# Routing stage of an expert layer: the router's product turned round, the register loads split around two gathers, fewer filler matmuls, an early Silu table, and the last norm's squares by pairs

## The reference, cut to what matters

```
def _rmsnorm_f32(x, g):
    xf = x.astype(jnp.float32)
    return xf * lax.rsqrt(jnp.mean(xf * xf, axis=-1, keepdims=True) + RMS_EPS) * g.astype(jnp.float32)
...
def _moe_swiglu(h, router_w, router_b, w_gate, w_up, w_down):
    hf = h.reshape(bsz * seq, d)
    logits = (hf @ router_w + router_b).astype(jnp.float32)
    probs = jax.nn.softmax(logits, axis=-1)
    top_p, top_i = lax.top_k(probs, TOP_K)
    top_p = top_p / jnp.sum(top_p, axis=-1, keepdims=True)
    gates = jnp.sum(jax.nn.one_hot(top_i, N_EXPERTS, dtype=jnp.float32) * top_p[..., None], axis=1)
    out = jnp.zeros_like(hf)
    for e in range(N_EXPERTS):
        out = out + gates[:, e:e + 1] * _swiglu(hf, w_gate[e], w_up[e], w_down[e])
    return out.reshape(bsz, seq, d)
```

## Time and profile before

| | us |
|---|---|
| median of 3 runs | 1529.41 |
| lowest, highest | 1526.29, 1532.66 |
| the profiled execution: its time | 1524.15 |
| the profiled execution: its span | 1522.3 |
| TensorE busy (matmuls) | 1437.0, 94% |
| routing, from the last norm's end to the first block | 589.4 to 618.2 |
| expert loop | 618.2 to 1501.8 |
| final sum, norm and output | 1501.8 to 1522.3 |

### The profile page before, as it was taken

One profiled execution on the slowest core, in us unless ns is written; L12 is line 12 of the kernel. 1 busy time (PEld: TensorE's weight loads), 2 busy tenths in 40 slices (PEclk: granted clock), 3 DMA queues, 4 the chain that ended last, 5 costly groups with the idle time before them and its releaser, 6 DMA issues.

```text
span 1522.3 us, 44793 instructions
## 1 busy us (share of the span) xinstructions
PE 1437.0 (94%) x19926; PEld 1087.0 (71%) x19926; DVE 371.7 (24%) x1020; ACT 158.5 (10%) x377; POOL 138.2 (9%) x230
## 2 busy tenths in 40 slices
PE   5998999999998899899999989989989999999997
PEld 4886788888887887666667767757757767765554
DVE  2815240220203714111111111111111111113334
ACT  2103111111012203100000000000000000000001
POOL 0000041240300000000000000000000000000000
PEclk9999999999999998999999999999999999999999
DMA  9948496656318805749999999999999999999860
GB/s 386 422 157 310 173 369 239 266 194 249 139 62 353 333 0 229 298 180 387 425 427 410 426 427 408 427 425 413 426 426 409 420 427 424 420 425 380 366 293 29
DMA packets 44203, 493.92 MB, mean 324 GB/s; under 512 B 4896, under 2 KB 5152, under 8 KB 5792
## 3 DMA queue, kind: packets, MB, share of 16 engines
q1 hardware_dynamic: 41040, 475.02, 76.0%
q10 hardware_dynamic: 3024, 16.73, 2.7%
HBM read 478.10 MB, written 13.63 MB: 323 GB/s over the span
## 4 chain that ended last, share of the span: by engine, by line
PE 81%; DMA 12%; DVE 4%; issue 1%; ACT 1%; POOLq 0%; SPq 0%; POOL 0%; DVEq 0%
PE PS L740 30%; PE PS L442 20%; PE PS L749 15%; DMA ring<-in_expert_stream 9%; PE PS L596 5%; DMA arena<-in_expert_stream 2%; PE PS L426 2%; DMA ring<-in_dense_stream 2%; PE PS L758 1%; DVE arena L1047 1%; PE PS L720 1%; PE PS L650 1%; PE PS L566 1%; PE PS L578 1%; PE PS L474 1%
## 5 line engine op out<-in xcount | busy, mean ns | idle before, releaser
L740 PE MATMUL PS<-ring,arena 128*32 128x256 f32 x7040 | 406.5, 381 | 26.2 <-DMA ring<-in_expert_stream 14.6
L740 PEld LDWEIGHTS PS<-ring,arena 128*32 128x32 f32 x7040 | 257.3, 110 | 154.1 <-issue 20.7
L442 PE MATMUL PS<-arena,ring 128*128 128x256 f32 x1408 | 313.4, 383 | 3.9 <-ACT arena L850 2.7
L442 PEld LDWEIGHTS PS<-arena,ring 128*128 128x128 f32 x1408 | 268.6, 192 | 44.4 <-issue 3.0
L749 PE MATMUL PS<-ring,arena 128*32 128x256 f32 x4928 | 298.3, 380 | 0.8 <-DVE consts L1047 0.8
L749 PEld LDWEIGHTS PS<-ring,arena 128*32 128x32 f32 x4928 | 183.8, 110 | 85.1 <-issue 3.1
L740 PE MATMUL PS<-arena 128*32 128x256 f32 x2816 | 162.1, 380 | 6.9 <-DMA arena<-in_expert_stream 4.8
L1047 DVE TENSOR_TENSOR stat<-stat,PS 128x128 f32<-128x128 f32 x154 | 44.2, 287 | 508.4 <-ACT stat L1004 508.4
L1047 DVE TENSOR_TENSOR arena<-arena,PS 128x256 f32 (+1 forms) x123 | 55.2, 449 | 372.2 <-PE PS L442 232.8
L740 PEld LDWEIGHTS PS<-arena 128*32 128x32 f32 x2816 | 106.3, 110 | 53.8 <-DMA arena<-in_expert_stream 5.8
L1595 POOL COPY arena<-arena 128x256 f32 x153 | 61.3, 401 | 812.6 <-PE PS L740 764.0
(11 more groups left out here) (183 smaller groups left out, 623.8 us busy)
## 6 DMA issues: line engine op xcount, KB each, us to landing
ring<-in_expert_stream SPq DMA_DIRECT2D x136, 2048.0 KB, 19.7
ring<-in_dense_stream SPq DMA_DIRECT2D x105, 1024.0 KB, 7.5
arena<-in_expert_stream SPq DMA_DIRECT2D x32, 2048.0 KB, 22.8
ssm_scratch<-arena ACTq DMA_DIRECT2D x12, 1024.0 KB, 4.9
ring<-ssm_scratch SPq DMA_DIRECT2D x12, 1024.0 KB, 9.7
arena<-in_xt ACTq DMA_DIRECT2D x1, 1024.0 KB, 13.7
arena<-in_ssm_small ACTq DMA_DIRECT2D x1, 1024.0 KB, 9.6
out_t<-arena ACTq DMA_DIRECT2D x4, 256.0 KB, 2.6
```

What stands on the lines that cost most here:

```text
L442: mm = pe.matmul(PS[:, bank, j * T:(j + 1) * T], w[:, c, j * P:(j + 1) * P], moving[:, c, :], start=(c == 0), stop=(c == NC - 1))
L740: mm = pe.matmul(PS[32 * q:32 * q + 32, 0, 0:256], hbuf[:, c * BLK:(c + 1) * BLK], w[:, q * 256:(q + 1) * 256], start=(c == 0), stop=(c == ...
```

## The change

It has five parts.

**Router's product.** The router's 8 columns become the stationary side and the chunk's 256 tokens the moving side: eight matmuls, one for each chunk, into a tile of 8 partitions x 256. DVE copies that to `logit_t` (a stretch of `reps`, free at that time), and TensorE turns it with two small matmuls against the 8 x 8 corner of the identity. The turning of the chunks, which lay between the products, comes behind them: the first four ahead of the turn of the logits, the other twelve behind it, and ACT copies them in the order 0, 1, 2, 3.

**Register loads.** TensorE loads four sums after the first gather and four after the second, instead of eight after the second. ACT loads its eight ahead of its two copies instead of behind them. POOL makes the first copy to `hbuf` when one group is gathered (`hg_ready` 1) instead of two.

**Fillers.** Both spins of nine become spins of three.

**Silu table.** ACT runs a Silu on two columns right behind the Exp of the routing, into a tile that is overwritten later. On DVE the three small steps that turn this Exp into the gates stand behind the `sel` matrices.

**Squares by pairs.** ACT's squares of the final norm wait for `e_x` 1, 2, 3 and 4 one by one, instead of all for 4.

The diff, cut to its core:

```diff
+        logit_t = reps[:, 256:512]
...
             for c in range(NC):
                 pe.wait_ge(h_ready, 3 * NC + c + 1)
-                for tt in range(2):
-                    mm = pe.matmul(PS[:, 5, tt * 8:tt * 8 + 8], H[:, c, tt * P:(tt + 1) * P],
-                                   cols[:, K_RW + 8 * c:K_RW + 8 * c + 8], start=(c == 0 and tt == 0), stop=(c == NC - 1),
-                                   skip_group_check=True)
-                if c == NC - 1:
+                mm = pe.matmul(PS[0:EXPERTS, 5, 0:T], cols[:, K_RW + 8 * c:K_RW + 8 * c + 8], H[:, c, :], start=(c == 0), stop=(c == NC - 1))
+            mm.then_inc(logits_turned, 1)
+            for m in range(4):
+                if m == 1:
+                    pe.wait_ge(logits_taken, 1)
+                    for tt in range(2):
+                        mm = pe.matmul(PS[:, 2, 32 + 8 * tt:40 + 8 * tt], logit_t[0:EXPERTS, tt * P:(tt + 1) * P], ident[0:EXPERTS, 0:EXPERTS],
+                                       start=True, stop=True)
                     mm.then_inc(logits_ready, 1)
-                for tt in range(2):
-                    m, i = (tt * NC + c) // 4, c % 4
+                for i in range(4):
+                    tt, c = (4 * m + i) // NC, (4 * m + i) % NC
                     mm = pe.transpose(PS[:, (6, 7, 0, 1)[m], i * P:(i + 1) * P], H[:, c, tt * P:(tt + 1) * P], ident)
-                    if i == 3:
-                        mm.then_inc(htm_psum, 1)
+                mm.then_inc(htm_psum, 1)
...
-            spin(9, 3)
+            spin(3, 3)
             pe.wait_ge(htm_ready, 4)
             gather(0)
+            pe.wait_ge(items_ready, 1)
+            upto = blocks_upto(pe, range(EXPERTS // 2))
             gather(1)
-            pe.wait_ge(items_ready, 1)
-            upto = blocks_upto(pe)
+            upto += blocks_upto(pe, range(EXPERTS // 2, EXPERTS))
...
-            spin(9, 2)
+            spin(3, 2)
             sums(4, 0)
...
             act.activation(r2[5], r2[4], ACT.Exp).then_inc(pick_exp, 1)
+            act.activation(e_act_b[:, 0:2], r2[4], ACT.Silu)
...
+            act.wait_ge(items_ready, 1)
+            upto = blocks_upto(act)
             take_gathered(0)
             take_gathered(1)
-            act.wait_ge(items_ready, 1)
-            upto = blocks_upto(act)
...
-            act.wait_ge(e_x, 4)
-            squares(4, lambda cp: None)
+            squares(4, lambda cp: act.wait_ge(e_x, cp + 1))
...
+            dve.wait_ge(logits_turned, 1)
+            dve.tensor_copy(logit_t[0:EXPERTS], PS[0:EXPERTS, 5, 0:T]).then_inc(logits_taken, 1)
             dve.wait_ge(logits_ready, 1)
-            link(tt(logit, PS[:, 5, 0:16], cols[:, K_RB:K_RB + 16], ALU.add))
+            link(tt(logit, PS[:, 2, 32:48], cols[:, K_RB:K_RB + 16], ALU.add))
...
-            pool.wait_ge(hg_ready, GATHERED[0])
+            pool.wait_ge(hg_ready, 1)
             pool.tensor_copy(hbuf, hg[:, 0:256]).then_inc(hbuf_ready, 1)
             for e in range(EXPERTS):
-                if e:
-                    pool.wait_ge(hg_ready, GATHERED[e])
+                pool.wait_ge(hg_ready, GATHERED[e])
```

More of the change, by code:

```diff
@@ L305, in trunk_kernel @@
         (y_laid, yd_ready, gelu_ready, sig_ready,) = [sem(n) for n in "y_laid yd_ready gelu_ready sig_ready".split()]
-        (logits_ready, htm_psum, htm_ready, picked_ready, gap_ready,) = [sem(n) for n in "logits_ready htm_psum htm_ready picked_ready gap_ready".split()]
+        (logits_turned, logits_taken, logits_ready, htm_psum, htm_ready, picked_ready, gap_ready,) = [sem(n) for n in "logits_turned logits_taken logits_ready htm_psum htm_ready picked_ready gap_ready".split()]
         (pick_exp, pos_ready, items_ready, places_ready, sel_ready,) = [sem(n) for n in "pick_exp pos_ready items_ready places_ready sel_ready".split()]
@@ L344, in gap_cell, with blocks_upto @@
             return PS[:, 3, n * P:(n + 1) * P]
-        def blocks_upto(eng):
-            return [eng.value_load(items[0:1, e:e + 1], min_val=LEAST * (e + 1), max_val=UPTO[e]) for e in range(EXPERTS)]
+        def blocks_upto(eng, experts=range(EXPERTS)):
+            return [eng.value_load(items[0:1, e:e + 1], min_val=LEAST * (e + 1), max_val=UPTO[e]) for e in experts]
         block = ctx.enter_context(nc.Block())
@@ L986, in _ @@
             shift(3)
-            for n, m in enumerate((0, 2, 1, 3)):
+            for n, m in enumerate(range(4)):
                 act.wait_ge(htm_psum, n + 1)
@@ L1411, in _ @@
             tt(r2[4], r2[2], r2[0], ALU.subtract).then_inc(gap_ready, 1)
[L1412 to L1415, removed]
             dve.wait_ge(pos_ready, 1)
@@ L1447, in _ @@
                 s.then_inc(sel_ready, 1)
+            dve.wait_ge(pick_exp, 1)
+            link(dve.tensor_scalar(r2[6], r2[5], 1.0, None, ALU.add))
+            link(dve.reciprocal(r2[6], r2[6]))
+            link(tt(r2[7], r2[5], r2[6], ALU.mult))
             for k, src in enumerate((slot_of[0], slot_of[1], r2[6], r2[7])):
```

## The result

The changed kernel takes 1516.85 us (median of five runs, 1516.15 to 1520.79); the kernel before 1529.41 (1526.29 to 1533.33). The ratio is 0.9933, with a 95% interval of 0.9916 to 0.9949: 0.5 to 0.8% faster. The profiled execution took 1516.15.

The account below looks back on a forecast made before the run. The weight stream was taken to bound the expert loop from about 700 us, its start set by TensorE. Routing 4.0 plus last norm 2.5 gave 6.5 us off the 1529.41 median: 1522.9 us, range 1518 to 1527.5.

Parts of the forecast that it names:

- What bounds the kernel: Expert loop: the weight stream bounds from about 700 us, TensorE sets its start; an earlier first block moves the end equally.
- register loads: Around TensorE's gathers: two groups of four loads leave 1.5 us idle each, 3.0 instead of 3.44 (bounds 1.0 and 4.6).
- Case A: Routing: clock low for part of the first gather, which takes 6.1 us; 1519.5 to 1526 us, chance 0.50.
- case B: Routing: clock stays or returns early, first gather at full clock, first block 6.4 us sooner; 1520.5 us, chance 0.25.
- C: Routing: both gathers at the low clock, nothing gained ahead of the loop, 2.5 in the last norm; 1526.9 us, chance 0.13.
- E: Expert loop: clock stays low into its blocks, each slow block costing 5.5 us more; kernel slower, chance 0.05.
- The product: Router's product: new form lets DVE start on the logits at 594.0 instead of 595.66, 1.6 us sooner.
- Fillers: Ahead of the first gather: TensorE's fillers lost 3.4 us; six records instead of eighteen end ahead of `sel`.
- Last norm: Final norm: squares by pairs and fewer fillers bring the root at 1511.3 instead of 1513.83, 2.5 us sooner (bounds 1.1, 2.8).
- The table load: Last norm: by the skill's drain of about 1.38 us beside the 1.28 load, root at 1512.7, gain 1.1; taken as lower bound.
- The early Silu table: Silu's table load of 1.28 us was hidden ahead of the first block's end; its removal is worth nothing.

Follow-up runs that it names:

- e5: Changed kernel with 45 fillers instead of three ahead of the first gather; first block 36.96 us behind the router's first product, total 1534.85 us.
- e3: Changed kernel with TensorE's eight register loads back behind the second gather; first block starts 23.07 us behind the router's first product, ends 28.42.
- e12: Changed kernel with four register loads ahead of the first gather, four between the gathers, and eight fillers instead of three; 1516.95 us, ratio to before 0.9914.
- e7: Changed kernel with nine fillers instead of three ahead of the last norm's sums, squares by pairs kept; first residual step to root 7.51 us.
- e10: Changed kernel executed again without edit, as a control; first block starts 22.65 us behind the router's first product, ends 26.31.
- e6: Changed kernel with the last norm's squares waiting for all residuals again, three fillers kept; first residual step to root 7.69 us.
- e9: Kernel before executed again without edit, as a control; first block starts 26.17 us behind the router's first product, ends 31.52.
- e11: Kernel before with three fillers instead of nine ahead of the first gather; first block starts 24.42 us behind the router's first product, ends 30.98.
- e1: Changed kernel with the old router product and its order of transposes put back; first block starts 22.41 us behind the router's first product.
- e4: Changed kernel with nine fillers instead of three ahead of the first gather; first block starts 21.43 us behind the router's first product.

## Why the prediction was right or wrong

**What bounds the kernel: right.** That TensorE's start of the loop sets the stream of weights and that a microsecond ahead of it is one at the end was argued from the still DMA; e5 shows it with a delay of 15.8 us.

**The size: too small.** I said 6.5 us, own time 1517.65, and 1522.9 against the median. The stretches give 7.6 + 2.3 = 9.9 in the recorded pair and about 6.2 + 2.4 = 8.6 over all the executions (last norm: mean 8.2 over the four with the old form, 5.8 over the eight with the new one). The ratio of the timed runs gives 10.2 (7.8 to 12.8). The median, 1516.85, lies 6.0 below my forecast and 1.2 below the low end of my range. I gave 0.57 to "within 0.5%" and 0.38 to "faster by over 0.5%"; the second came true, narrowly.

Term by term, for the recorded pair's routing (4.0 forecast, 7.6 measured): the first gather starts 0.3 later than forecast, takes 3.81 us instead of 6.1 (2.3 gained), the two pauses take 1.21 instead of 3.0 (1.8 gained), and the second gather 3.83 instead of 3.66 (0.2 lost). The 2.3 is the clock, which in this execution happened to hold. The 1.8 is the loads, and at least as much comes in every execution of the changed kernel in which the two pauses can be read.

**The step that failed: the register loads.** "I take 1.5 each, 3.0 instead of 3.44", a gain of 0.4. The two idle times are 0.68 and 0.53 at the full clock and 0.21 and 0.51 behind a slow gather: 1.2 and 0.7. The term is worth 1.9 (e3), and with the first block's clock 3.6 in that pair. I had taken the price of a load from POOL, 0.57, which left 1.1 us hidden for the eight on TensorE, and then not even counted on that much for each group of four. The mechanism was right, a hidden part for each group; its size was wrong. From 3.40 for eight (e3) and 0.53 for four, and if the same time is hidden for each group, one gets an estimate of 0.72 for a load and 2.3 hidden. e12 agrees: four loads behind the sums at 601.59 would end near 604.6, and its gather starts at 604.76. That TensorE's load is dearer than POOL's 0.57 is an inference from these, not measured by itself.

**The clock.** Case A (0.50) had the clock low for part of the first gather, case B (0.25) kept it. The recorded execution is B: my B put the first block 22.3 us behind the first product (611.7 less 589.4), it came at 21.14. e7 and e10 are A nearly to the letter (gathers of 5.84 and 5.79 us, 6.1 forecast, ended 18.1 us behind the first product as forecast), e6 lies between. So both were right as mechanisms, and which one comes differs between executions. C, with both gathers slow throughout, was not seen. What E feared, a slow block at the start of the loop, was seen in small, and not in the changed kernel: it came behind the long pause, in e9, e11 and e3. My argument against E, that "a pause of 3.44 us before the first block did not lower the clock", was true of one trace and of two executions in five with such a pause. This step was wrong: the change takes the long pause away and with it the slow first block, 1.7 us in e9, a gain that I did not count. It is no part of the recorded pair, whose first blocks both take 3.66.

The section "HAM oscillation — how this bites in real kernels" of "TensorE: Matmul & The Clock Gate" in the Trainium skill, from which I had rival C, tells of waits for transfers that are longer than the bursts of matmuls they part. I had laid it on the two new pauses, which are far shorter than the gathers beside them: at most 0.71 us in the eight executions, and the clock fell behind none of them. The pause that is like the section's waits is the one of before, 3.4 us, and there the trace agrees in three executions of five. So it did not speak against the change, since the change takes away the longest pause.

**The product: right in size, wrong in what it is good for.** 1.6 us sooner at DVE was forecast, 1.48 measured; the counts 2.8 sooner forecast (598.0 against 600.79), 2.58 measured; first gather at 12.0, measured 12.29. But e1 shows that against an old product at the full clock the gain is 0.2 at the logits and 1.2 at the gather: most of the 1.48 was the low clock, which had hit the product in the recorded trace and in none of the three other executions of the old product (e1, e9, e11), where it fell behind it.

**Fillers: right for the one trace, too simple as a cause.** "To the fillers" I put the 3.4 us that the gather waited. At the full clock nine of them would have cost 0.3 (e4); in the second execution of before they ended 2.7 us sooner behind the first product than in the first. What cost the time was fillers at half the clock behind a late count.

**Last norm: right.** 2.5 forecast, 2.34 measured, by the mechanism named, and both halves are needed as the text had it (e6, e7). That the clock can fall here too, as it did in e10, I had not weighed; it costs up to 0.9 us there. The table load: the section "What ACT_TABLE_LOAD costs" of "ScalarE: Activation LUTs" in the Trainium skill would have put the root 1.4 later; the changed kernel shows 1.28 for the load, and the root 1.45 behind its start, 0.16 of it waiting for the sums. No drain is to be seen. The early Silu table brought nothing that shows, as forecast: from the first block to the second it is 4.46 us in both kernels. It was not tried alone, and neither were ACT's and POOL's part of the change.

## What to carry to other kernels

In this kernel TensorE's register loads were partly hidden behind what the engine had queued, and anew for each group: split between two gathers they left 1.2 us idle instead of 3.4, and behind the short pauses the clock never fell, where behind the long one it often did. Two edits that each free one of two things a step waits for can be worth next to nothing apart and everything together, so try them together. And one trace shows one course of the clock: before a forecast rests on where it fell, look at a second execution, or give a range for both.

## What the runs showed of the hardware

The granted clock takes different courses in executions of the same kernel: low from 3 to 17 us or from 6 to 13 behind the first product in the kernel before, not at all or from 9.5 to 16 in the changed one. With a pause of 3.4 us behind two unbroken gathers the clock fell in the pause or within 1.1 us of its end in three of five executions, and cost 1.7 to 2.9 us in the first block. With pauses of at most 0.71 us between the same matmuls it fell behind none, in eight executions.

The part ahead of the routing, the same in all of these kernels, ended anywhere within 5.9 us. The timed runs of the kernel before lie 7.0 us apart, and ten more that were made beside e12 lie 11.0 apart (1524.34 to 1535.30, one run of 7084.83 left out). The part ahead of the routing can give a good part of that; the loop, from 886.7 to 892.4 us, and the last norm, from 7.70 to 9.19, add theirs.
